# Modulation sums taken out of an attention stage into two dense stages, and a stream's inputs formed in fewer passes

## The reference, cut to what matters

```python
def ada_mod(cond, w, b):                       # block 2: cond is c_2 or c_ctx_2, w is 1024 x 6144, two layers
    m = (silu(cond) @ w + b)[..., None, :]
    return jnp.split(m, 6, axis=-1)            # sh1, sc1, g1, sh2, sc2, g2

def modulate(h, shift, scale):
    return h * (1 + scale) + shift

# layer 0 of block 2, for the latent and the context stream
h = modulate(rms_norm(x, norm1_g), sh1, sc1)
x = x + g1 * ab_mixer(h)                       # gated MLP over chunks, gated delta rule
x = x + g2 * conv_ffn(modulate(rms_norm(x, norm2_g), sh2, sc2))
# layer 1 of block 2, ends with the latent stream only
h = modulate(rms_norm(x, norm1_g), sh1, sc1)
x = x + g1 * (block_attention(q, k, v) @ w_out)      # 8 heads, 512 queries, 768 keys
x = x + g2 * conv_ffn(modulate(rms_norm(x, norm2_g), sh2, sc2))
```

## The kernel before, in words

| stage | before | after |
|---|---|---|
| p_hgrn_mm (12 output tiles) | 12 x 2 | 12 x 3 |
| pool_mm | 2 x 1 | 2 x 1 |
| u_mm | 11 x 2 | 11 x 2 |
| w_out | 8 x 1 | 8 x 1 |
| a_in (25 output tiles) | 6 x 2 | 8 x 2 and 12 x 1 |
| attention (32 iterations) | 28 x 1 | none |

## Time and profile before

### The profile page before, as it was taken

How to read it: one execution, slowest core, us unless ns; L and a number is a source line. 1 busy time by engine, 2 the same in 40 slices (tenths; PEclk the granted TensorE clock), 3 DMA queues, 4 the chain that set the end, 5 groups by cost and what they waited for, 6 DMA issues and landing times. The chain is left out here.

```text
span 3370.3 us, 59977 instructions
## 1 busy us (share of the span) xinstructions
PE 2729.0 (81%) x24570; PEld 2198.3 (65%) x24570; DVE 1534.7 (46%) x2390; ACT 1040.4 (31%) x1562; POOL 825.0 (24%) x479
## 2 busy tenths in 40 slices
PE   2568666948758588996878779999998989789998
PEld 2565444837748456885768668888886733467886
DVE  6766724763363376415354334404413277345142
ACT  2331211232132144344212344312224422255232
POOL 3311102303104022220211222322241200234444
PEclk9787758969869788998989899999998988899999
DMA  4420003510000045120000311212212222223222
GB/s 169 151 86 1 1 38 141 182 42 3 3 1 4 20 156 194 44 69 28 3 2 4 125 44 62 66 59 62 67 52 75 85 75 75 81 75 94 93 96 85
DMA packets 61452, 228.71 MB, mean 68 GB/s; under 512 B 5953, under 2 KB 12225, under 8 KB 59201
## 3 DMA queue, kind: packets, MB, share of 16 engines
q1 hardware_dynamic: 61248, 225.76, 19.2%
HBM read 212.10 MB, written 13.63 MB: 67 GB/s over the span
## 5 line engine op out<-in xcount | busy, mean ns | idle before, releaser
L2474 POOL TENSOR_TENSOR f_wl<-f_stage,f_wh 128x1024 fp32r<-128x1024 f32 (+1 forms) x120 | 316.3, 2636 | 615.3 <-ACT f_wh L2470 615.3
L2470 ACT ACTIVATE f_wh<-f_stage 128x1024 fp32r<-128x1024 f32 (+1 forms) x120 | 137.8, 1148 | 592.2 <-PE f_ps L2563 591.0
L2563 PE MATMUL f_ps<-h_h,f_wh 128*128 128x256 f32 (+1 forms) x704 | 238.7, 341 | 16.9 <-POOL f_wl L2474 12.4
L2563 PE MATMUL f_ps<-h_h,f_wl 128*128 128x256 f32 (+1 forms) x704 | 238.0, 340 | 0.0
L2563 PE MATMUL f_ps<-h_l,f_wh 128*128 128x256 f32 (+1 forms) x704 | 237.7, 340 | 0.0
L2768 DVE SCALAR_TENSOR_TENSOR f_xr<-f_ps,cols,f_xr 128x511 f32<-128x511 f32 (+1 forms) x132 | 83.1, 657 | 337.9 <-ACT f_xr L2761 337.4
L2563 PE MATMUL f_ps<-f_f_ah,f_wh 128*128 128x512 f32 (+1 forms) x528 | 183.6, 355 | 0.0
L2563 PE MATMUL f_ps<-f_f_ah,f_wl 128*128 128x512 f32 (+1 forms) x528 | 183.5, 354 | 0.0
L2563 PE MATMUL f_ps<-f_f_al,f_wh 128*128 128x512 f32 (+1 forms) x528 | 183.4, 354 | 0.0
L2563 PEld LDWEIGHTS f_ps<-h_h,f_wh 128*128 128x128 f32 x704 | 132.9, 189 | 35.3 <-POOL f_wl L2474 13.5
L2563 PE MATMUL f_ps<-hc_h,f_wh 128*128 128x512 f32 x352 | 142.0, 403 | 13.2 <-POOL f_wl L2474 13.0
(11 more groups left out here) (683 smaller groups left out, 6930.2 us busy)
## 6 DMA issues: line engine op xcount, KB each, us to landing
f_stage<-in_ffn_up SPq DMA_DIRECT2D x88, 512.0 KB, 3.5
f_stage<-in_ffn_down SPq DMA_DIRECT2D x32, 704.0 KB, 4.0
att_side_w<-in_ada_w SPq DMA_DIRECT2D x28, 512.0 KB, 3.2
a_in_stage<-in_ab_w SPq DMA_DIRECT2D x25, 512.0 KB, 3.3
p_hgrn_mm_side_w<-in_ada_w SPq DMA_DIRECT2D x12, 1024.0 KB, 4.8
u_mm_side_w<-in_ada_w SPq DMA_DIRECT2D x11, 1024.0 KB, 4.9
mod_w<-in_mod_w SPq DMA_DIRECT2D x8, 1024.0 KB, 13.9
p_hgrn_mm_stage<-in_w_in SPq DMA_DIRECT2D x12, 512.0 KB, 4.8
```

What stands on the lines that cost most here:

```text
L2470: self.nc.scalar.activation(self.wh[:, slot, :w], self.stage[:, slot, :w], ACT.Copy).then_inc(self.w_high, 1)
L2474: self.nc.gpsimd.tensor_tensor(self.wl[:, slot, :w], self.stage[:, slot, :w], self.wh[:, slot, :w].bitcast(F32), ALU.subtract).then_inc(se ...
L2563: done = self.nc.tensor.matmul(out[s][:, :tn], w, x[:, k, t0:t0 + tn], start=k == 0 and n == 0, stop=k == job.kt - 1 and n == 2)
```

## The change

Five things change:

1. The attention loses its SP queue, the silu of the vectors and its 28 sums, and the modulation stage behind it goes: the one ahead of ab_out now covers features 48 to 95.
2. `p_hgrn_mm` sums three tiles of `ada_w` beside each output tile, not two. The later stages' first tiles shift by 12.
3. `a_in` sums two tiles beside each of its first eight output tiles (before: beside tiles 2 to 7), and one tile beside each of the 12 q, k, v tiles, in the same buffers. On SP the side loads stand between the weight loads; the transposes and mixes of the gated MLP are moved one job back on each engine.
4. `Feed` forms xr = (x·scale)·root on DVE, xh = xr + shift on ACT and xl = (xr + shift) - xh on DVE. Nothing unrounded is stored. DVE works span by span, two instructions a pass.
5. In `w_out` the context input is loaded one job sooner, squared after job 1 and summed on PE ahead of job 3 (before: after it).

```diff
@@ class Gemv
-    def place(self, st):
-        self.rows = st.sbuf("side_w", [P, 2, self.per, D])
...
+    def place(self, st, name="side", room=None):
+        self.rows = room.rows[:, :, :self.per, :] if room else st.sbuf(f"{name}_w", [P, 2, self.per, D])
...
@@ class Feed, on_dve
         def scaled(k):
             if k >= self.RING:
-                dve.wait_ge(self.high_ok, k - self.RING + 1)
-                self.wait_full(dve, k - self.RING)
-            self.nc.vector.tensor_tensor(self.xr[:, k % self.RING, :], self.x[:, k, self.lo:self.hi], self.root[:, :], ALU.mult
-                                         ).then_inc(self.xr_ok, 1)
...
+                dve.wait_ge(self.low_ok, k - self.RING + 1)
+            for s, (t0, n) in enumerate(self.spans):
+                ins = self.nc.vector.scalar_tensor_tensor(self.part(k, s), self.x[:, k, t0:t0 + n], self.scale(k, s),
+                                                          self.root[:, t0 - self.lo:t0 - self.lo + n], ALU.mult, ALU.mult)
+            ins.then_inc(self.xr_ok, 1)
         def low(k):
             dve.wait_ge(self.high_ok, k + 1)
-            self.wait_full(dve, k)
-            self.nc.vector.tensor_tensor(self.xl[:, k, self.lo:self.hi], self.full[:, k % self.RING, :],
-                                         self.xh[:, k, self.lo:self.hi].bitcast(F32), ALU.subtract).then_inc(self.low_v, 1)
+            for s, (t0, n) in enumerate(self.spans):
+                ins = self.nc.vector.scalar_tensor_tensor(self.xl[:, k, t0:t0 + n], self.part(k, s), self.shift(k, s),
+                                                          self.xh[:, k, t0:t0 + n].bitcast(F32), ALU.add, ALU.subtract)
+            ins.then_inc(self.low_ok, 1)
@@ class Feed, on_act
-                ins = self.nc.scalar.activation(self.xh[:, k, t0:t0 + n], self.part(self.xr, k, s), ACT.Identity,
-                                                scale=self.scale(k, s), bias=self.shift(k, s))
+                ins = self.nc.scalar.activation(self.xh[:, k, t0:t0 + n], self.part(k, s), ACT.Identity, bias=self.shift(k, s))
             ins.then_inc(self.high_ok, 1)
-            if k in self.FULL_BY_DVE:
-                continue
...
@@ first_out
-                if j == 2:
+                if j == 1:
                     sp.dma_start(x3[:, :, :CTX], d["ctx_2"]).then_inc(ctx_in, 16)
...
-            for job in jobs[1:]:
+            for job in jobs[1:3]:
                 row.products(pe, job)
             pe.wait_ge(ctx_squared, 1)
...
             done.then_inc(ctx_ok, 1)
+            row.products(pe, jobs[3])
...
-                if job is jobs[2]:
+                if job is jobs[1]:
@@ branch_flow, SP
+            for g in range(2):
+                row.load_one(sp, to_v[0], g, g, False)
             side.load_vec(sp)
+            for g in range(2):
+                side.load(sp, g, g)
             row.load(sp, to_v[1])
             gmlp.load(sp)
             sp.dma_start(x_dram, x3[:, :, :]).then_inc(kept, 16)
-            for job in row.jobs[2:-2]:
+            for job in to_u:
                 row.load(sp, job)
+            for g in range(8, 20):
+                row.load_one(sp, to_qkv[g // 2 - 4], g, g % 2, False)
+                if g == 10:
+                    sp.wait_ge(side.used, 10)
+                if g >= 10:
+                    late_side.load(sp, g - 10, g % 2)
+            for i in range(10, 12):
+                late_side.load(sp, i, i % 2)
+            row.load(sp, to_ab)
@@ branch_flow, PE (ACT and DVE alike)
             row.products(pe, to_qkv[0])
+            row.products(pe, to_qkv[1])
             gmlp.transposes(pe)
-            row.products(pe, to_qkv[1])
+            row.products(pe, to_qkv[2])
             gmlp.mixes(pe)
@@ attention
-        @block.sync
-        def _(sp):
-            side.load_vec(sp)
-            for n in range(n_side):
-                side.load(sp, n, n % 2)
...
-            side.silu(nc, act)
             exponential(0)
...
-                if n < n_side:
-                    side.sums(nc, dve, n, n % 2)
@@ second
-            modulation(nc, t, "mods2", 48, cols_of(t, "ada_b_2")[:, 48:68], (56,), (gains1[:, KD:],))
+            modulation(nc, t, "mods2", 48, cols_of(t, "ada_b_2")[:, 48:], (56, 80), (gains1[:, KD:], gains2[:, KD:]))
...
-        modulation(nc, t, "mods2", 68, cols_of(t, "ada_b_2")[:, 68:], (80,), (gains2[:, KD:],))
@@ build, dense(nc, "p_hgrn_mm", ...)
-                      side=Gemv(d["ada_w"], d["vec_2"], mods2, 0, 2))
+                      side=Gemv(d["ada_w"], d["vec_2"], mods2, 0, 3))
```

More of the change, by code:

```diff
@@ L2675, in on_dve @@
                 scaled(k)
-            if k and k - 1 in self.FULL_BY_DVE:
-                full(k - 1)
-            if k and k - 1 not in self.LOW_BY_POOL:
+            if k:
                 low(k - 1)
@@ L2915, in ffn_flow @@
         xr, full = st.sbuf("xr", [P, 3, w]), st.sbuf("full", [P, 3, w])
-        feed = Feed(nc, st, x, KD, lo, T, root, *mods_of(mods, o, [j for _, _, j in conds]), hh, hl, xr, full)
+        feed = Feed(nc, st, x, KD, lo, T, root, *mods_of(mods, o, [j for _, _, j in conds]), hh, hl, xr)
         rms = Rms(nc, t, st, "rms", x, KD, lo, T, 1e-6, root, sq=xr[:, 0:2], acc=full[:, 1])
@@ L2955, in _ @@
         def _(pool):
-            feed.on_pool(pool, range(0, 1))
             row.low(pool, 0, 0, KD * P)
-            feed.on_pool(pool, range(1, KD))
             row.low(pool, 1, 1, KD * P)
@@ L3122, in _ @@
             row.low(pool, 0, 0, KD * P)
-            feed.on_pool(pool, range(KD))
             row.low(pool, 1, 1, KD * P)
@@ L3535, in branch_flow @@
         vtok = ring[:, 0:4, :].rearrange("p f t -> p (f t)").rearrange("p (i f) -> p i f", i=TT)
-        feed = Feed(nc, st, x3, KD, 0, T, root, *mods_of(mods, 0, (1, 0)), hh, hl, ring[:, 0:3, :], ring[:, 3:6, :])
+        feed = Feed(nc, st, x3, KD, 0, T, root, *mods_of(mods, 0, (1, 0)), hh, hl, ring[:, 0:3, :])
         side.place(st)
+        late_side.place(st, "late_side", side)
         gate = side.rows[:, :, :, :].rearrange("p a b d -> p (a b d)")[:, :GW * T].rearrange("p (f t) -> p f t", t=T)
@@ L3577, in silu @@
                 nc.scalar.activation(tile, tile, ACT.Silu).then_inc(silu_ok, 1)
-            return Job(d["ab_w"], A_QKV + base, n_tiles, KD, hh, hl, SEGS, act=act_out, dve=dve_out, post=silu)
-        to_v = [Job(d["ab_w"], A_V + a, 2, KD, hh, hl, SEGS, act=out(v, a, ACT.Gelu), side=side if a else None, side_from=2)
+            return Job(d["ab_w"], A_QKV + base, n_tiles, KD, hh, hl, SEGS, act=act_out, dve=dve_out, post=silu,
+                       side=late_side, side_from=8)
+        to_v = [Job(d["ab_w"], A_V + a, 2, KD, hh, hl, SEGS, act=out(v, a, ACT.Gelu), side=side)
                 for a in (0, 2)]
-        to_u = [Job(d["ab_w"], A_U + a, 2, KD, hh, hl, SEGS, act=out(u, a, ACT.Gelu), side=side, side_from=2) for a in (0, 2)]
+        to_u = [Job(d["ab_w"], A_U + a, 2, KD, hh, hl, SEGS, act=out(u, a, ACT.Gelu), side=side) for a in (0, 2)]
         to_qkv = [taps(base, 2) for base in range(0, 12, 2)]
@@ L3638, in _ @@
             act.wait_ge(kept, 16)
-            row.on_act(act, to_qkv[0])
+            for job in to_qkv[:2]:
+                row.on_act(act, job)
             gmlp.copy_on_act(act)
-            for job in (*to_qkv[1:], to_ab):
+            for job in (*to_qkv[2:], to_ab):
                 row.on_act(act, job)
@@ L3660, in _ @@
             side.credits(dve)
+            late_side.credits(dve)
             feed.on_dve(dve)
             dve.wait_ge(side.vec_ok, 1)
-            row.on_dve(dve, to_v[1])
-            row.on_dve(dve, to_u[0])
+            for job in (*to_v, to_u[0]):
+                row.on_dve(dve, job)
             gmlp.center(dve)
@@ L3667, in _, with attention @@
             gmlp.normalise(dve)
-            row.on_dve(dve, to_qkv[0])
+            for job in to_qkv[:2]:
+                row.on_dve(dve, job)
             gmlp.copy_on_dve(dve)
-            row.on_dve(dve, to_qkv[1])
+            row.on_dve(dve, to_qkv[2])
             gmlp.gates(dve)
-            for job in to_qkv[2:]:
+            for job in to_qkv[3:]:
                 row.on_dve(dve, job)
             units.scale(dve)
-def attention(nc, t, qn, qr, kn, kr, vtok, oh, ol, side, n_side):
+def attention(nc, t, qn, qr, kn, kr, vtok, oh, ol):
     QT = LAT // P
@@ L3704, in attention @@
         o_ps = st.banks("o", 2)
-        side.place(st)
         block = st.block()
-        @block.sync
-        def _(sp):
-            side.load_vec(sp)
-            for n in range(n_side):
-                side.load(sp, n, n % 2)
         @block.tensor
```

87 lines of the change are left out of this document (23 added, 64 removed).

## The result

The changed kernel took 3336.07 us in the median of four runs (3335.24 to 3340.94); the kernel before, with one more run, 3380.97 (3370.83 to 3405.64). The ratio on record is 0.9902 with a 95% interval of 0.9875 to 0.9928. It isn't the quotient of these two medians (0.9867, or 44.9 us), of which the second rests on four runs up to 35 us apart. In the three later sets of 7 to 13 runs the kernel before had medians of 3370.5 to 3373.4 us. In the last of them the changed kernel ran again: 3342.43 against 3373.42 us, 31 us apart, with a ratio of 0.9903 (0.9875 to 0.9932). The forecast was 3340 (3320 to 3362), with a chance of 0.52 for a gain of over 1% and of 0.42 for less; the gain of 0.98% by the ratio lies just on the side of the second. The span of the profiled execution went from 3370.3 to 3334.6 us, that is by 35.7, to the tenth the sum that was forecast.

The account below looks back on a forecast made before the run. PE was taken to bound the kernel overall, with DVE's sums setting the pace in the attention. The terms summed to -35.7 us, 3336.4 by the profiled execution and 3343.8 by the median, taken as 3340 (3320 to 3362).

Parts of the forecast that it names:

- -41.3 forecast for the 28 gaps: Attention iterations: 22 plain gaps of 3.97 us and 6 of 9.17 take 142.4 us, not 183.7.
- the start -3.0 forecast: Attention start: without vectors and silu the first exponential comes earlier, -3.0 us, between 0 and -3.2.
- the stage gone behind it -1.6 forecast: Between attention and c_out: one modulation stage and its barrier go, -1.6 us (0 to -2.4).
- but for the clock: Attention iterations: PE's work is unchanged, so the time can't go below 142.4 us except through PE's clock.
- -3.3, -3.0 and -1.3 forecast: Feeds in the FFN of layer 0, c_in and last FFN: tile 1's first product comes that many us sooner.
- 12 x 7.45 + 10 x 2.2: p_hgrn_mm: DVE's twelve steps of six sums, ten lengthened by POOL's low part, 111.4 us; the stage +14.7.
- The upper bound: p_hgrn_mm: at most +18 us, with all of POOL's 2.93 on every step and a late last weight.
- I give back 1.8 of it: a_in, first tiles: side loads hold the third and fourth weight tile, leaving -1.1 us of the feed's 2.9.
- Rival B: a_in: side loads waiting for sums hold weight loads, five tiles at 3 us each; total -21, 3355 us; chance 0.12.
- the prediction's own sign for B: a_in: PE waits for weights over 5 us together would show Rival B.
- +2.5 forecast: a_in, where PE waits for DVE's gates: late sums of 2.3 us stand ahead of them, +2.5 us.
- Rival D: Stages DVE now paces: PE's clock falls towards half, p_hgrn_mm +89 us; total +53, 3429 us; chance 0.08.

Follow-up runs that it names:

- the half-sums kernel: The kernel before with one of the two sums of each tile (the second condition's) left out in the attention: 3337.66 us, ratio 0.9897.

## Why the prediction was right, and where it was wrong

*Attention: right.* -41.3 forecast for the 28 gaps, 142.4 against 183.7 measured, -41.2; the start -3.0 forecast: the first exponential now stands 4.7 us behind PE's first matmul (7.8 before), -3.1, of which 2.8 show in the row maxima; the stage gone behind it -1.6 forecast, and 0.85 us now lie between (2.45 before), -1.6. The step that carried it, reading the last iterations of the stage, in which the sums had run out, is what made it exact: the profile of before held a piece of the kernel after. What I had put only in a side remark ("but for the clock") is two thirds of the mechanism: 26.9 of the 41.2 us are PE's slower clock, and the half-sums kernel shows that with pauses of 0.40 us and less the clock stays at 1.00.

*Feeds: right.* -3.3, -3.0 and -1.3 forecast in the FFN, c_in and the last FFN; -3.8, -3.4 and -1.2 measured between the first DVE operation and tile 1 (the stretch of c_in lost 3.6). In a_in 2.9 was forecast; the feed alone gave 3.4 by that distance and 4.2 in the stretch. The chain (ACT's last high part, tile 1's high part, POOL's low part) was the right one.

*p_hgrn_mm: mechanism right, one term mis-sized.* "12 x 7.45 + 10 x 2.2": ten of the twelve steps meet a low part, as said, but such a sum takes 2.9 us (2.86 at 136.26, mean of ten 2.87), not 3.42, so it costs 1.65 and not 2.2. 12 x 7.45 + 10 x 1.65 is 105.9, and DVE's sums ran 106.0 us. That is 5.5 of the 5.6 that were forecast too much. I had taken the one row at 134.51 for all; when DVE has no pause it meets the low part at another point, further into it. PE did not slow to 9.3 us a tile at once, as forecast: from 134.10 to 184.15 its tiles stood 8.34 apart, on the stock of loaded weights, then 9.0 to 9.1 with pauses of 0.5 us, and the one pause of 2.01 us came at the end (221.99). The upper bound was summed wrongly: 2.93 in place of 2.2 on ten steps is 7.3 us more, not 3, so it should have been +22.

*a_in, first part: wrong.* The step was "I give back 1.8 of it". PE waits 2.68 and 2.88 us for the weights of tiles 3 and 4, and behind these pauses the clock of 0.50 makes the two tiles 3.3 us longer: 9.0 instead of 1.8. Four more executions of this part paused 0.5 to 1.9 and 4.0 to 6.2 us there. The right queue and the right tiles were named, and the price was put under the size of one pause, because the stock of two tiles was counted as cover. But the load of tile 3 stands behind the first four sums, which end at 1310.3 because they begin only behind the feed, and by then PE is at the end of tile 1. The store of x ahead of tile 4's weights, 13.6 us to their landing, was in no term. Rival B had the mechanism, at 3 us a tile for five tiles; it was two tiles and the clock. By the prediction's own sign for B, waits for weights of over 5 us together in a_in, it came true: 6.5 us behind the first tile.

*a_in, second part: right in place* and in size for the mixes (+2.5 forecast, +2.6 measured); for the transposes +1.3 was forecast and +0.7 came. On top came 0.6 us at the tile behind q, k and v, whose weight load stands behind the last side loads (ACT waits 7.46 us for it), which I hadn't seen, and the clock behind the pauses. In all +5.5 in this execution and up to +7.9 in others of the same code, where +3.8 was forecast.

*w_out.* 0 with bounds of 1.5 was forecast; 1.8 in the two profiles, likely about 1.

*Rival D* (PE falls to its lower clock in the stages that DVE paces) was wrong where I had put it: in p_hgrn_mm PE's pauses were 0.5 us and the clock stayed at 1.00 from 134 to 214; it fell to 0.50 only from 223.20 to 226.61, behind the one pause of 2 us. But the sentence that no row of the kernel before shows a drop after a pause of 1 us was a misreading of its own trace, which has it in the attention at or just behind the end of each of five pauses of 1.0 us and six of 1.55 (0.98 us before 2710.14, then 0.50). The Trainium skill, "TensorE: Matmul & The Clock Gate", § HAM oscillation — how this bites in real kernels, has pauses between groups of matmuls lower the clock; the trace agrees for the pauses of 2.0 to 2.9 us in a_in, in w_out and in p_hgrn_mm and for those of 1.0 to 1.6 us in the attention of before. It does not for those of 0.8 and 0.9 us in a_in before 1302.70, behind which the clock was 1.00 until 1322.29, nor in every case for longer ones: 1.84 us before 1533.06 left it at 1.00, and so did 2.66 us in one of eight profiles of w_out.

*The sum* hit because p_hgrn_mm (5.6 too dear) and the gated delta rule's 5.5 stood against a_in (7.7 too cheap) and w_out (1.8). In the later set the medians lie 31 us apart and the ratio gives 33; the touched stages sum to 32.6.

## What to carry to other kernels

Side work that waits for its turn in an in-order queue has two prices: its own time where it stands ahead of what another engine waits for, and the time by which it holds the loads that are queued behind its own loads. Most of both hangs on the order alone: the same sums cost 13 us less in a_in when each side load stood one weight load later, the store of x too, and when copies and gates stood ahead of the sums. Before moving work off a bottleneck ask whether it must be done: 32 of these 192 sums were never read. And look in the profile for a stretch where the moved work had already run out; here it gave the new pace to 0.1 us (142.4 forecast and measured).

## What the runs showed of the hardware that I had not expected

- A pause of PE can cost more than itself. In w_out sixteen matmuls took 7.13 us after 1.44 us of idle time, in all five profiles, and 8.6 to 8.8 after 2.66, in seven of eight (7.13 in the eighth). In a_in two pauses of 2.7 and 2.9 us were each followed by a short stretch at 0.50, and cost 3.3 us beyond their own 5.6. In the kernel with half of the sums a pause of 2.6 us at the start gave 17 us at 0.50, which is 8.5 us. In the attention of before 14.4 us of pauses came with 26.9 us of slower work.
- Short and regular pauses can do either: with PE busy 19.6 of 20 us the attention ran at 1.00, with PE busy 24.4 of 27 at 0.87 in the mean, in turns of 1.00 and 0.50.
- An operation of DVE with two inputs in SBUF that meets one of POOL does not always pay the same: 3.42 us in one case and 2.86 in another, for 1.23 alone. It pays for what is left of POOL's operation when it begins, and then 1.1 us of its own (1.08 or 1.09 in all nineteen such sums of p_hgrn_mm, nine before and ten after): in the earlier trace rows POOL ends at 136.85, 2.34 us behind the start at 134.51, which gives 3.42; in the changed kernel POOL ends at 138.04, 1.78 us behind the start at 136.26, which gives 2.86.
- Untouched stages wander from execution to execution on the same code: the gated delta rule from 316.0 to 324.8 us, rwkv from 488.2 to 495.8. Each wanders by some 8 us, so an effect of that size is not to be read from two profiled spans, but well from the stretch in which it lies.
